# A hybrid attention layer: order of steps in the up-projection, the opening of chunked attention, group B's scores, and the first visit of the out-projection

## The reference, cut to what matters

```python
h = rms_norm(x, g_in)
(a_q, a_k, a_v, a_gate, b_cq, b_ckv, b_kr, b_gate, m_q, m_gate) = jnp.split(h @ w_in, points, axis=-1)
out_a = swa_sink_attention(qa, ka, va, a_sinks) * jax.nn.silu(a_gate)
qb = (rms_norm(b_cq, b_g_cq) @ b_w_q_up).reshape(b, s, B_HEADS, B_NOPE + B_ROPE)
kvb = (rms_norm(b_ckv, b_g_ckv) @ b_w_kv_up).reshape(b, s, B_HEADS, B_NOPE + B_V)
sc = (jnp.einsum('bqhd,bkhd->bhqk', qn, k_nope)
      + jnp.einsum('bqhd,bkd->bhqk', qr, k_rope)).astype(jnp.float32) * scale
out_b = mla_attention(qb_nope, qb_rope, kb_nope, kb_rope, vb) * jax.nn.silu(b_gate)
out_m = memory_cross_attention(qm, km, vm) * jax.nn.silu(m_gate)
return x + jnp.concatenate([out_a, out_b, out_m], axis=-1) @ w_o
```

## Time and profile before

| | |
|---|---|
| Median of 3 runs | 1497.71 us (1497.15 to 1497.88) |
| The profiled execution | 1495.54 us, of which the span 1493.7 us |
| PE matmul busy | 1456.3 us (97%) |
| DVE, ACT, POOL busy | 675.8 (45%), 472.0 (32%), 97.6 us (7%) |
| Chain that ended last, by engine | PE 86%, ACT 6%, DVE 5%, issue 2%, DMA 1% |

### The profile page before, as it was taken

One profiled execution on the slowest core, in us unless ns is written; L12 is line 12 of the kernel. 1 busy time (PEld: TensorE's weight loads), 2 busy tenths in 40 slices (PEclk: granted clock), 3 DMA queues, 4 the chain that ended last, 5 costly groups with the idle time before them and its releaser, 6 DMA issues.

```text
span 1493.7 us, 18069 instructions
## 1 busy us (share of the span) xinstructions
PE 1456.3 (97%) x7142; PEld 1196.8 (80%) x7142; DVE 675.8 (45%) x1072; ACT 472.0 (32%) x850; POOL 97.6 (7%) x78
## 2 busy tenths in 40 slices
PE   9999999999999999999999999789999899999999
PEld 7888888888888888888788788556788688888887
DVE  4333241342514131302225867896668744444443
ACT  4450311313030121101224544894557411111111
POOL 1011000201101000000001122110000000000000
PEclk9999999999999999999999999999999999999999
DMA  9541231121123131121353621551012233333223
GB/s 360 195 112 57 99 112 42 46 109 56 42 98 113 43 113 42 56 98 56 121 189 103 225 66 45 138 146 49 8 29 72 71 113 106 106 113 94 90 83 115
DMA packets 52927, 146.81 MB, mean 98 GB/s; under 512 B 5632, under 2 KB 9728, under 8 KB 51584
## 3 DMA queue, kind: packets, MB, share of 16 engines
q1 hardware_dynamic: 42352, 101.21, 21.1%
q0 software_dynamic: 10368, 44.73, 8.3%
q10 hardware_dynamic: 144, 0.02, 0.0%
HBM read 117.61 MB, written 28.32 MB: 98 GB/s over the span
## 4 chain that ended last, share of the span: by engine, by line
PE 86%; ACT 6%; DVE 5%; issue 2%; DMA 1%; POOL 0%; ACTq 0%; SPq 0%; DVEq 0%
PE ps L1581 25%; PE ps L1583 25%; PE ps L1582 25%; ACT a_p L836 2%; PE ps L1819 2%; PE ps L1783 2%; PE ps L1800 1%; PE ps L1782 1%; PE ps L1786 1%; DVE ss L1280 1%; ACT u_fin L795 1%; PE ps L1635 1%; PE ps L1634 0%; PE ps L1825 0%; ACT b_pT L855 0%
## 5 line engine op out<-in xcount | busy, mean ns | idle before, releaser
L975 DVE TENSOR_TENSOR w_lo<-w_raw,w_hi 128x1024 fp32r<-128x1024 f32 x87 | 106.6, 1225 | 503.0 <-ACT w_hi L629 502.8
L629 ACT ACTIVATE w_hi<-w_raw 128x1024 fp32r<-128x1024 f32 x89 | 94.2, 1059 | 592.9 <-PE ps L1583 571.6
L1581 PE MATMUL ps<-w_hi,h_hi 128*128 128x512 f32 x640 | 249.1, 389 | 1.1 <-DVE h_lo L990 1.1
L1583 PE MATMUL ps<-w_hi,h_lo 128*128 128x512 f32 x640 | 249.0, 389 | 0.0
L1582 PE MATMUL ps<-w_lo,h_hi 128*128 128x512 f32 x640 | 249.0, 389 | 0.0
L1581 PE MATMUL ps<-h_hi,w_hi 128*128 128x512 f32 x512 | 199.2, 389 | 0.0
L1582 PE MATMUL ps<-h_lo,w_hi 128*128 128x512 f32 x512 | 199.2, 389 | 0.0
L1583 PE MATMUL ps<-h_hi,w_lo 128*128 128x512 f32 x512 | 199.2, 389 | 0.0
L1582 PE MATMUL ps<-mixed_lo,z_hi 128*128 128x512 f32 x384 | 149.4, 389 | 0.0
L1581 PEld LDWEIGHTS ps<-w_hi,h_hi 128*128 128x128 f32 x640 | 120.2, 188 | 26.3 <-issue 1.5
L1583 PEld LDWEIGHTS ps<-w_hi,h_lo 128*128 128x128 f32 x640 | 120.2, 188 | 25.1
(11 more groups left out here) (279 smaller groups left out, 2081.2 us busy)
## 6 DMA issues: line engine op xcount, KB each, us to landing
w_raw<-in_w SPq DMA_DIRECT2D x89, 512.0 KB, 3.5
z<-in_w_out SPq DMA_DIRECT2D x64, 256.0 KB, 2.6
x_nat<-in_x POOLq DMA_DIRECT2D x8, 1024.0 KB, 8.5
xq<-in_xT SPq DMA_DIRECT2D x32, 256.0 KB, 4.3
out_y<-xq SPq DMA_DIRECT2D x32, 256.0 KB, 3.4
x_raw<-in_xT SPq DMA_DIRECT2D x7, 1024.0 KB, 18.5
gate_s<-T POOLq DMA_DIRECT2D x3, 2048.0 KB, 7.0
mixed<-gate_s POOLq DMA_DIRECT2D x12, 512.0 KB, 5.2
```

The source lines that it names most:

```text
L629: a.activation(w_hi[:, n % SPLIT, :], w_raw[:, n % RAW, :], ACT.Copy).then_inc(hi_ready, 1)
L975: v.tensor_tensor(w_lo[:, n % SPLIT, :], w_raw[:, n % RAW, :], w_hi[:, n % SPLIT, :].bitcast(F32), ALU.subtract).then_inc(lo_ready, 1)
L1581: mm(out, a_hi, b_hi, start=start, stop=False)
L1583: return mm(out, a_lo, b_hi, start=False, stop=stop)
```

## The change

It moves calls; no instruction is added or taken away, and no buffer or semaphore changes.

In the up-projection, ACT rounds the next input (`up_in`) before it squares the tile before (`up_square`), and DVE keeps `knT` and makes `c_lo` before it sums the squares (`up_squares`). At the opening of chunked attention, ACT turns to chunk 0's queries before the last square, and loads the exponential's table before the last tile's products. Group B's score of two pieces is written by kind: both pieces with `kr_high`, both with `kr_low`, both with `knT`. In the out-projection's first visit, `left_high(3, ...)` goes from c = 2 to c = 3 behind `z_high(4)`, `left_low` is cut in two halves that stand elsewhere (`left_low(2, 0)` ahead of `z_low(2)`, the other calls behind `z_make`), and the residual's loads go from behind `load_z(2)` to behind `load_z(4)`.

```diff
@@ -494,7 +494,7 @@
                 load_mq(t, t % 2)
             for c in range(2, NOUT):
                 load_z(c)
-                if c == 2:
+                if c == 4:
                     load_xq(0)
                 if c >= NUNIT and c % NUNIT == 3:
                     store_y(c // NUNIT - 1)
@@ -875,19 +875,21 @@
             for step in range(TT):
                 if step >= 1:
                     up_in(step)
+                if step >= 2:
+                    up_square(step - 2)
+                if step >= 1:
                     up_out(step - 1)
                 if step >= 3:
                     up_keep(step - 3)
-                if step >= 1:
-                    up_square(step - 1)
-
+
+            up_square(TT - 2)
             keys_kept()
+            bring_in(ACT.Exp)
             up_out(TT - 1, between=memory_keys_kept)
+            turn_q(A, 0, 0)
             up_square(TT - 1)
-            turn_q(A, 0, 0)
             up_keep(TT - 3)
             turn_q(A, 1, 1)
-            bring_in(ACT.Exp)
             up_keep(TT - 2)
             exponents(A, 0, 0)
             turn_q(A, 2, 0)
@@ -946,13 +948,13 @@
                 visit = c // NUNIT
                 if 2 <= c + 1 < NOUT:
                     z_high(c + 1)
+                if c == 3:
+                    left_high(3, 0)
+                    left_high(3, 1)
                 if c in (1, 3, 4):
                     k = {1: 10, 3: 12, 4: 14}[c]
                     plain_high(k)
                     plain_high(k + 1)
-                if c == 2:
-                    left_high(3, 0)
-                    left_high(3, 1)
                 if c % NUNIT == 6:
                     act.wait_ge(summed, 7 * visit + 1)
                     wait(act, x_added, visit)
@@ -1407,13 +1409,12 @@
                                        .to_broadcast([P, MH, NMEM]), ALU.mult)
 
             for step in range(TT):
-                if step >= 1:
-                    up_squares(step - 1)
                 if step >= 3:
                     up_keep(step - 3)
                 if step + 1 < TT:
                     up_in(step + 1)
                 if step >= 1:
+                    up_squares(step - 1)
                     up_norm(step - 1)
 
             up_keep(TT - 3)
@@ -1548,6 +1549,10 @@
                 if u == 0 and visit >= 1:
                     for q in range(3):
                         finish(visit - 1, q)
+                if c == 0:
+                    plain_low(8)
+                    plain_low(9)
+                    left_low(2, 0)
                 if 2 <= c + 1 < NOUT:
                     z_low(c + 1)
                 if u == 0 and visit >= 1:
@@ -1555,19 +1560,21 @@
                 if c == 2:
                     left_sums(3, 0)
                     left_sums(3, 1)
-                if c in (0, 2, 4, 5):
-                    k = {0: 8, 2: 10, 4: 12, 5: 14}[c]
+                if c in (2, 4, 5):
+                    k = {2: 10, 4: 12, 5: 14}[c]
                     plain_low(k)
                     plain_low(k + 1)
-                if c in (1, 3):
-                    left_low(2 + c // 2, 0)
-                    left_low(2 + c // 2, 1)
                 if u == 6:
                     partial_sums(visit)
                 if u == 7:
                     add_sums(visit)
                 if c + 2 < NOUT:
                     z_make(c + 2)
+                if c == 1:
+                    left_low(2, 1)
+                if c == 3:
+                    left_low(3, 0)
+                    left_low(3, 1)
             for q in range(4):
                 finish(NVISIT - 1, q)
 
@@ -1774,13 +1781,13 @@
                 elif at_ is B:
                     h, t = BSTEPS[c]
                     q, width = slice(t * P, (t + 1) * P), (t + 1) * P
-                    for a in range(0, width, HALF):
-                        b = min(width, a + HALF)
-                        out = ps[:, bank + a // HALF, 0:b - a]
-                        wide = max(b, a + 256)
-                        for kr, start in ((kr_high, True), (kr_low, False)):
+                    pieces = [(a, min(width, a + HALF)) for a in range(0, width, HALF)]
+                    for kr, start in ((kr_high, True), (kr_low, False)):
+                        for a, b in pieces:
+                            wide = max(b, a + 256)
                             mm(ps[:, bank + a // HALF, 0:wide - a], qr[h // 2][:, h % 2, q], kr[:, a:wide], start=start, stop=False)
-                        ins = mm(out, qnT[:, h, q], knT[:, h, a:b], start=False, stop=True)
+                    for a, b in pieces:
+                        ins = mm(ps[:, bank + a // HALF, 0:b - a], qnT[:, h, q], knT[:, h, a:b], start=False, stop=True)
                 else:
                     for h in range(MH):
                         ins = mm(ps[:, bank + h // 2, h % 2 * NMEM:(h % 2 + 1) * NMEM], c_qT[:, par, h, :], kmT[:, h, :],
```

## The result

The change takes **1487.96 us** (median of 4 runs, 1485.94 to 1489.54), the kernel before 1497.45 (4 runs, 1497.15 to 1497.88): a ratio of 0.9936, 95% interval 0.9922 to 0.995, 9.5 us less. I had forecast 1490.5 and a range down to 1488.0. Yet the profiled execution of the change took 1487.98 us with a span of 1486.2, where I had 1488.3 and 1486.5. So the sum came out on the one trace and not on the medians, and the question of this study is why.

What follows compares the result with a forecast made beforehand. PE was taken as the bound (97% busy), with ACT setting the pace in steady chunked attention. Gains 1.7 + 0 + 0 + 0 + 5.5 = 7.2 us off the 1497.7 median gave 1490.5; range 1488.0 to 1494.0.

Steps and rivals of the forecast that it cites:

- Up-projection: Steady tiles: DVE's chain 9.6 us instead of 9.97 and setting the pace, PE 2.7 us sooner by the last tile.
- Last normalisation: End of the up-projection: DVE's last normalisation ends 1.8 us sooner, taken as 1.7; bounds 0.5 and 2.7.
- Chunk 0's queries: Opening of chunked attention, queries before the last square: gain nothing; the wait for the last normalisation grows to about 6.3 us.
- the table load: Opening of chunked attention, exponential's table loaded earlier: gain nothing, as chunk 1 needs PE's last turn behind the same wait.
- group B: Group B's scores by kind: at most 0.3 us, taken as 0.
- Out-projection: First visit: PE's three waits for the low part of the weights go, 5.5 us won; bounds 3.0 to 5.6.
- The clock: Half-clock stretch behind the wait for the last normalisation: effect of -1 to +1.3 us, taken as 0.
- My own sign of being wrong: Opening of chunked attention: the forecast is wrong if the half-clock stretch is much longer than 7 us.
- Rival 1: Up-projection: DVE keeps up with PE, all 2.7 us arrives, clock perhaps another 1: 8.2 to 9.5 less; chance 0.13.
- Rivals 2 to 5: First visit keeps a wait, 0.12; opening gives nothing, 0.07; clock makes it slower, 0.03; nothing measurable, 0.05.
- Rival 4: Chunked attention: the clock does not come back after 6.3 us of standing, kernel slower, up to 1525; chance 0.03.

Runs made afterwards that it cites:

- e8: The change with DVE keeping the non-rotary keys (`knT`) after the squares, while POOL takes the roots, in the up-projection: 1485.12 us, ratio 0.9922.
- e5: The change without the opening's two edits (chunk 0's queries and the table load back in their old places): 1488.15 us, ratio 0.9937.
- e3: The kernel before with only the opening's two edits (chunk 0's queries and the table load moved): 1496.31 us, ratio 0.9998.
- e4: The kernel before with only group B's scores ordered by kind: 1496.10 us, ratio 0.9998.
- e6b: The kernel before with 26 unused transposes added on PE in the wait for the last normalisation: 1493.37 us, ratio 0.9986.
- e2: The kernel before with only the edits of the out-projection's first visit: 1491.90 us, ratio 0.997.
- e0: The change run once more, unaltered, against the kernel before: 1487.51 us, ratio 0.9933.
- e10: The change with 28 instead of 22 transposes at PE's start: 1488.48 us, ratio 0.9943.
- e6: The change with 40 unused transposes added on PE in the long wait for the last tile's normalisation: 1486.55 us, ratio 0.9927.

## Why the prediction was right, and where it was not

**Up-projection: right.** DVE's chain 9.6 forecast, 9.58 measured; PE's wait for `c_lo` shrank and did not vanish; by the end of the tiles PE was 2.9 us sooner (2.7 forecast). The reason given for it, work of DVE's that POOL's roots no longer hide, is shown by e8, which hides it again and has 8.91.

**Last normalisation: 1.7 was too little.** Against a start that lay equally, the wait ended 2.12 us sooner, and 2.10 to 2.20 in four other profiles with this order (1.83 in e5). No one row is off: with the start made equal, the last sums of squares began 2.1 us sooner (forecast 1.8), some 0.1 in each of three steps, and I had taken 0.1 off.

**Chunk 0's queries, the table load, group B: nothing, right.** The wait became 5.8 us (6.3 forecast), e3 and e4 moved no median by over 0.8 us, and their intervals hold 1.

**Out-projection: 5.5 forecast, 5.56 measured** against the same profile. But that profile had the longest first visit of five with the old order (3.4 us of waits in e6b, 4.6 before), so the typical gain is smaller: 5.1 on their average, 4.9 at the medians of e2. I had written that no transfer in this list was late; yet ACT stood 4.49 us for the weights of c = 2, and that landing set where DVE's list began.

**The clock: -1 to +1.3 forecast, -1.31 to +0.62 measured** for the change, e0 and e10. I had it go by when in the wait the clock falls. It fell during the wait in all three, and what differed is how long it stayed down, 10.2 us in the change and in e10 and 6.8 in e0; what decides that isn't shown. My own sign of being wrong, a stretch at half much longer than 7 us, is there in two of three profiles. "For which I take 0" was the middle and no more than that; in the profile of the change it was a loss of 0.6, which swallowed the 0.4 by which the normalisation did better than forecast, while PE had come to the up-projection 0.6 sooner, for no edit's sake. So the close agreement on the one trace, 1487.98 against 1488.3, was partly luck: -7.56 was made of -2.12, -5.56, +0.62, -0.61 and +0.11.

**The step that failed** is one line: "The median of the runs is 1497.71, 2.2 us above it; I take differences from the trace off the median." That treats the 2.2 us as a constant, and they are not. Over 54 runs the kernel before lay between 1493.29 and 1500.61. Of the first 30 of these, five at a mean clock of 0.998 averaged 1494.5, eight at 0.995 1497.0, three at 0.993 1499.1: the time goes with how long the clock stood at half, about 0.75 us for each 0.001. (That is a correlation. A mean clock lower by 0.001 is 3 us more at half, and at 0.37 us lost for each of these it would be 1.1.) The profile of before had 0.998, its 54 runs average 0.996, so a typical run of before paid some 1.5 us more than the profile that I counted on. The nine runs of the change average 0.9970, and its profile had 0.996: that profile was as quick as a typical run, the one of before quicker. So the clock puts 0.8 us on top of the edits; with 2.1 and 4.9 to 5.6 for these it makes 7.8 to 8.5 us. The medians showed 9.5 and 9.8 (and 7.8 for e10, the same but for six transposes), each with an interval of some 2 us to either side. One line through all 63 runs of the two kernels, time against mean clock with a step between them, makes the step 8.4 us at equal clock, 7.7 to 9.1. What lies between the edits' 7.0 to 7.7 and these 8.4 stays open: it is inside the intervals, and e6 against e6b, made to settle it, has both answers in it.

**The range.** It was built from the bounds of the edits alone. Two medians of three or four runs, of kernels whose single runs lie over 3 us apart, add a microsecond or more each way. With that the range would have reached to 1487 or below. Rival 1 had the size (8.2 to 9.5) but the wrong reason: DVE did not keep up with PE. Rivals 2 to 5 fell. Rival 4's danger, a clock that does not come back, showed in no profile; 12.3 us at half behind the wait was the most.

## What to carry to other kernels

When a profiled execution is quicker than the median of its kernel, look for what differs between executions (here the mean granted clock in each run, and how much half clock stands behind PE's long waits) before a difference is put against the median, and put that spread into the range. Where PE must wait for several microseconds at a place behind which its own work is on the path, idle work that fits in the wait can be worth as much as a reordering: it gave 2 to 3 us in the kernel before, and in the change some 1 us at the medians, which the runs can't tell from nothing. And when a step is moved to come sooner, look at what the old place hid; e8 kept both merits, and its last normalisation came another 3.1 us sooner.

## What the runs showed of the hardware

- The same instructions behind the same wait paid from 1.2 to 4.4 us for the clock (3.0 to 12.3 us at half). It was not the wait's length that decided (3.5 us in the earlier trace rows, then 6.8 at half; 5.8 in the change, 7.9; 5.8 in e0, 3.0). Nor does it take a wait that long: in e5 the clock fell a microsecond behind one of 1.94 us.
- The Trainium skill (TensorE: Matmul & The Clock Gate, section What's actually happening) says that one kernel meets the slower level for a different number of matmuls in different runs. The runs agree: e0 and the change are the same program. It adds, of the slow start alone, that it costs under 1% of a typical kernel's span. Here the clock behind one wait costs 0.1 to 0.3%, as large as what this change can be judged by.
- At half clock a float32 transpose of 128x128 started every 0.21 us, at full every 0.11 (the 40 in 4.58 us); a 128x512 matmul took 0.63 and 0.39.
- Before the first rounded inputs arrive PE waited 0.9 to 3.1 us in executions of the same instructions, and four of thirteen profiles had some 3.4 us at half clock there. A 128x512 matmul started every 0.43 us in it and every 0.23 behind it, so 3.4 us at half lose some 1.6. Their 400th matmul came 1.7 to 2.9 us later than in the profile of before; in the other nine it lay within 0.7 of it.
